# Where the moving operands begin in their partition: another place in each of five rounds of x and in both perceptrons

## The reference, cut to what matters

```python
def sq_relu_mlp(h, w_up, w_down):
    return jnp.square(jax.nn.relu(h @ w_up)) @ w_down

x = x + mix
x = x + sq_relu_mlp(rms_norm(x, norm_mlp_g[layer]), mlp_w_up[layer], mlp_w_down[layer])
```

## Time and profile before

| | |
|---|---|
| Median of three runs | 860.49 us (859.25 to 860.76) |
| The profiled execution's own time | 859.15 us |
| Its span | 857.3 us |
| TensorE busy | 851.0 us, 99% |
| VectorE busy | 652.8 us, 76% |
| ScalarE busy | 496.0 us, 58% |
| Instructions | 17572, of which 7192 matmuls |

### The profile page before, as it was taken

How to read it: one execution, slowest core, us unless ns; L and a number is a source line. 1 busy time by engine, 2 the same in 40 slices (tenths; PEclk the granted TensorE clock), 3 DMA queues, 4 the chain that set the end, 5 groups by cost and what they waited for, 6 DMA issues and landing times.

```text
span 857.3 us, 17572 instructions
## 1 busy us (share of the span) xinstructions
PE 851.0 (99%) x7192; PEld 832.9 (97%) x7192; DVE 652.8 (76%) x1245; ACT 496.0 (58%) x905; POOL 46.8 (5%) x63
## 2 busy tenths in 40 slices
PE   9999999999999999999999999999999999999998
PEld 8999999999999899989999999999999999999998
DVE  6978678898978688575667555566799899997873
ACT  5785787764435667577778444443546564544650
POOL 0000000000000047000000000031020000000000
DMA  9927877878978623367657855617555323565541
GB/s 301 342 66 242 256 238 259 263 267 274 311 245 277 213 99 99 99 204 238 193 178 221 242 188 197 196 51 185 165 167 183 113 75 99 164 206 191 155 147 50
DMA packets 162864, 164.22 MB, mean 192 GB/s; under 512 B 16816, under 2 KB 159328, under 8 KB 162528
## 3 DMA queue, kind: packets, MB, share of 16 engines
q1 hardware_dynamic: 161696, 162.05, 59.7%
q10 hardware_dynamic: 1088, 1.05, 0.4%
HBM read 162.01 MB, written 2.91 MB: 192 GB/s over the span
## 4 chain that ended last, share of the span: by engine, by line
PE 94%; DVE 3%; ACT 1%; DMA 1%; issue 1%; POOL 0%; ACTq 0%; DVEq 0%
PE ps L316 24%; PE ps L318 24%; PE ps L320 24%; PE ps L442 3%; PE ps L1594 2%; PE ps L1596 2%; PE ps L1592 2%; PE ps L1653 2%; PE ps L459 2%; PE ps L1688 1%; PE ps L1692 1%; PE ps L1690 1%; DVE wl L283 1%; PE ps L1634 1%; PE ps L1643 1%; PE ps L1132 1%
## 5 line engine op out<-in xcount | busy, mean ns | idle before, releaser
L283 DVE TENSOR_TENSOR wl<-raw,wh 128x1024 fp32r<-128x1024 f32 x256 | 309.2, 1224 | 27.9 <-ACT wh L276 27.7
L316 PE MATMUL ps<-xh,wh 128*128 128x256 f32 x1136 | 320.2, 282 | 1.6 <-ACT xh L390 1.6
L318 PE MATMUL ps<-xl,wh 128*128 128x256 f32 x1136 | 315.6, 278 | 0.4
L320 PE MATMUL ps<-xh,wl 128*128 128x256 f32 x1136 | 315.4, 278 | 0.0
L276 ACT ACTIVATE wh<-raw 128x1024 fp32r<-128x1024 f32 x256 | 266.9, 1051 | 69.8 <-PE ps L320 62.5
L316 PEld LDWEIGHTS ps<-xh,wh 128*128 128x128 f32 x1136 | 213.8, 188 | 4.1 <-ACT xh L390 2.0
L318 PEld LDWEIGHTS ps<-xl,wh 128*128 128x128 f32 x1136 | 214.1, 188 | 1.2 <-DVE xl L384 1.0
L320 PEld LDWEIGHTS ps<-xh,wl 128*128 128x128 f32 x1136 | 213.5, 188 | 0.0
L320 PE MATMUL ps<-hh,wl 128*128 128x256 f32 x512 | 141.3, 276 | 0.0
L316 PE MATMUL ps<-hh,wh 128*128 128x256 f32 x512 | 141.3, 276 | 0.0
L318 PE MATMUL ps<-hl,wh 128*128 128x256 f32 x512 | 141.3, 276 | 0.0
(11 more groups left out here) (358 smaller groups left out, 1415.0 us busy)
## 6 DMA issues: line engine op xcount, KB each, us to landing
raw<-in_w_in_dram SPq DMA_DIRECT2D x34, 1024.0 KB, 5.4
raw<-in_mlp_up_dram SPq DMA_DIRECT2D x32, 1024.0 KB, 5.4
raw<-in_mlp_down_dram SPq DMA_DIRECT2D x32, 1024.0 KB, 7.3
aw<-in_w_adaT_dram SPq DMA_DIRECT2D x24, 512.0 KB, 4.8
raw<-in_rec_w_in_dram SPq DMA_DIRECT2D x7, 1024.0 KB, 11.6
raw<-in_att_w_in_dram SPq DMA_DIRECT2D x6, 1024.0 KB, 6.2
raw<-in_rec_w_out_dram SPq DMA_DIRECT2D x4, 1024.0 KB, 5.9
raw<-in_att_w_o_dram SPq DMA_DIRECT2D x4, 1024.0 KB, 5.0
```

What stands on the lines that cost most here:

```text
L283: e.tensor_tensor(parts_of(i)[1], raw_of(i), f32(parts_of(i)[0]), op=ALU.subtract).then_inc(S["wl"], 1)
L316: e.matmul(o, H[:, first + n], xh[:, k], start=start and n == 0, stop=False)
L318: e.matmul(o, H[:, first + n], xl[:, k], start=False, stop=False)
L320: ins = e.matmul(o, L[:, first + n], xh[:, k], start=False, stop=stop and n == len(ks) - 1)
```

## The change: what it does

`XH` and `XL` become five pairs of tiles, one for each round, and `HH`, `HL` get a place of their own in each layer. The pairs lie over each other in the same region, which has 512 bytes more. A round's two parts begin at 480, 96, 288, 352 and 224 within 512, the squared rows at 160 in layer 0 and at 416 in layer 1. All tiles that are placed behind move by 512 bytes. The order of instructions, the waits and the sizes are as before.

```diff
+X_AT = (480, 96, 288, 352, 224)
+HIDDEN_AT = (160, 416)
...
     align(top)
-    XH = place("xh", [128, 8, 256], F32R)
-    XL = place("xl", [128, 8, 256], F32R)
+    XH, XL = [], []
+    for r, past in enumerate(X_AT):
+        at_x = [top[0] + (past - top[0]) % 512]
+        XH.append(place(f"xh{r}", [128, 8, 256], F32R, at=at_x))
+        XL.append(place(f"xl{r}", [128, 8, 256], F32R, at=at_x))
+    top[0] += 16384 + 512
...
-        e.activation(XH[:, t], X[:, t], ACT.Copy, scale=gain).then_inc(S["xh"], 1)
+        e.activation(XH[r][:, t], X[:, t], ACT.Copy, scale=gain).then_inc(S["xh"], 1)
...
-            product(e, q, name, o, XH, XL, *of_x(0))
+            product(e, q, name, o, XH[0], XL[0], *of_x(0))
...
-    at_h = [ARENA]
-    HH = [place("hh0", [128, 32, 256], F32R, at=at_h)]
-    HL = [place("hl0", [128, 32, 256], F32R, at=at_h)]
-    at_h = [ARENA]
-    HH.append(place("hh1", [128, 32, 256], F32R, at=at_h))
-    HL.append(place("hl1", [128, 32, 256], F32R, at=at_h))
+    HH, HL = [], []
+    for l, past in enumerate(HIDDEN_AT):
+        at_h = [ARENA + (past - ARENA) % 512]
+        HH.append(place(f"hh{l}", [128, 32, 256], F32R, at=at_h))
+        HL.append(place(f"hl{l}", [128, 32, 256], F32R, at=at_h))
...
-        product(e, q, f"up{l}.{f}", o, XH, XL, *of_x(1 + 2 * l))
+        product(e, q, f"up{l}.{f}", o, XH[1 + 2 * l], XL[1 + 2 * l], *of_x(1 + 2 * l))
...
-        product(e, q, name, main(q, *freed)[:, 0:256], XH, XL, *of_x(2))
+        product(e, q, name, main(q, *freed)[:, 0:256], XH[2], XL[2], *of_x(2))
...
-        product(e, q, name, main(q, *freed)[:, 0:256], XH, XL, *of_x(4))
+        product(e, q, name, main(q, *freed)[:, 0:256], XH[4], XL[4], *of_x(4))
```

More of the change, by code:

```diff
@@ L383, in x_low @@
         q.wait_ge(S["xh"], 8 * r + t + 1)
-        e.scalar_tensor_tensor(XL[:, t], X[:, t], gain, f32(XH[:, t]), op0=ALU.mult, op1=ALU.subtract).then_inc(
+        e.scalar_tensor_tensor(XL[r][:, t], X[:, t], gain, f32(XH[r][:, t]), op0=ALU.mult, op1=ALU.subtract).then_inc(
             S["xl"], 1)
@@ L568, in vector_mixer @@
             q.wait_ge(S["xh"], t + 1)
-            e.tensor_tensor(XL[:, t], XG[:, t], f32(XH[:, t]), op=ALU.subtract).then_inc(S["xl"], 1)
+            e.tensor_tensor(XL[0][:, t], XG[:, t], f32(XH[0][:, t]), op=ALU.subtract).then_inc(S["xl"], 1)
         rms_variance(e, q, 0)
@@ L701, in scalar_mixer @@
             q.wait_ge(S["xg"], t + 1)
-            e.activation(XH[:, t], XG[:, t], ACT.Copy).then_inc(S["xh"], 1)
+            e.activation(XH[0][:, t], XG[:, t], ACT.Copy).then_inc(S["xh"], 1)
         q.wait_ge(S["rate"], 1)
@@ L1120, in tensor_q @@
         ks = range(4 * half, 4 * half + 4)
-        product(e, q, f"q{m}", ps[f"q{m}"], XH, XL, *of_x(2), ks=ks, first=4 * half, start=half == 0, stop=half == 1,
+        product(e, q, f"q{m}", ps[f"q{m}"], XH[2], XL[2], *of_x(2), ks=ks, first=4 * half, start=half == 0, stop=half == 1,
                 release=half == 1)
@@ L1468, in hybrid_two_block_kernel @@
     CTX_ROWS = (HCH, HCL, lambda k: (S["hch"], k + 1), lambda k: (S["hcl"], k + 1))
-    X_ROWS = (XH, XL, *of_x(4))
+    X_ROWS = (XH[4], XL[4], *of_x(4))
     V_ORDER = ((0, True), (0, False), (1, True), (1, False))
@@ L1795, in vector_modulated_low @@
         q.wait_ge(S["xh"], 32 + t + 1)
-        e.scalar_tensor_tensor(XL[:, t], T2.of[f"md{t}"][0][:], ADA[:, t:t + 1], f32(XH[:, t]), op0=ALU.add,
+        e.scalar_tensor_tensor(XL[4][:, t], T2.of[f"md{t}"][0][:], ADA[:, t:t + 1], f32(XH[4][:, t]), op0=ALU.add,
                                op1=ALU.subtract).then_inc(S["xl"], 1)
@@ L2087, in scalar_modulated @@
             q.wait_ge(S["mm"], done["up1.31"])
-            e.activation(XH[:, t], T2.of[f"md{t}"][0][:], ACT.Identity, bias=ADA[:, t:t + 1]).then_inc(S["xh"], 1)
+            e.activation(XH[4][:, t], T2.of[f"md{t}"][0][:], ACT.Identity, bias=ADA[:, t:t + 1]).then_inc(S["xh"], 1)
     def scalar_values2(e, q, n, blk):
```

## The result

The changed kernel took 872.60 us (median of four runs, 872.30 to 874.09), the kernel before 859.87 us beside it (859.12 to 860.76). The ratio is 1.0152, with a 95% interval of 1.0137 to 1.0166: 12.7 us slower. The forecast was 860.5 us with a range up to 868.0; the time lies outside it. The profiled execution took 872.43 us, its span is 870.6 us against 857.3.

The account below looks back on a forecast made before the run. It took TensorE's matmul pace to bound the kernel. Its terms, nothing for work on moved tiles and no pace change, summed to 0 us, so it forecast the median, 860.5 us, range 857.0 to 868.0.

Parts of the forecast that it names:

- What bounds the kernel: Whole kernel: TensorE busy 851.0 of 857.3 us, nobody else waited for; how fast matmuls follow each other sets the end.
- Step 1: ScalarE and VectorE writing and reading moved tiles: price nothing, bounds plus or minus 0.6 us.
- Step 2: Pace of the 3600 moved matmuls: three operand relations in the trace show no difference, so 0 us.
- That is a state, set at an entry and kept: In `product`: 113.3 or 117.8 ns between starts is chosen at an interruption and holds until the next.
- what would prove its reading wrong: Pace switching exactly where up products become down products, with no interruption, would mean the place itself sets it.
- Case B: Entries at 105.3 and 426.6 us fall to the slow pace, costing 6.6 or 4.9 us; likeliest 864 to 867; chance 0.33.
- the worst places: Outcomes left outside the range's upper end of 868.0 us, beside both long entries lost together.
- The upper bound of 13.3 us: All moved matmuls run slow: 2990 fast ones lose 4.45 ns each, 13.3 us.
- Case D: Moved matmuls below 113.3 ns, after the transposes' 109 ns; every second one gaining 4.3 ns gives 852.8 us; chance 0.07.
- The 0 us that the prediction drew from it: By the skill's account of engine ports, no place changes the matmul pace, so the sum is 0 us.
- The flag: In `product`: mean matmul length tells the pace without counting, 276 ns fast, 281 slow, anything else a third pace.
- The scatter of the runs: Three runs 1.5 us apart, worth 340 matmuls at the other pace; one entry at 383 us falling otherwise would do.

Follow-up runs that it names:

- the exchanged places: Changed kernel with weight parts at 224 and all streamed parts at 32, distance -192: 878.55 us, ratio 1.0215 to the kernel before.
- one stage at 96: Changed kernel with all moved tiles back at 224 except layer 0's up products at 96: 863.73 us, ratio 1.0050 to the kernel before.
- down products behind fast up products: Changed kernel, all rounds at 224, squared rows at 96 and 160: 866.87 us, ratio 1.0078; at 352 and 288: 867.48 us, 1.0085.

## Why the prediction was wrong

**What bounds the kernel** held. TensorE's matmuls follow each other without a wait before and after, and the whole loss is in their pace.

**Step 1, the work on the moved tiles, at nothing,** held: 509 and 426 ns against 510 and 426.

**Step 2, "Three relations, no difference. Value taken: no change of pace, 0 us", is the step that failed.** It measured 13.3 us of span. Its two supports were weak in the same way. The fp32 products of round 0 don't tell about the float32r ones: they start 216 ns apart at distance 192 and at 128, while `product` has 113.3 and 118.8 there. And `tensor_rows`, whose distance is -192 and whose pace was kept over a border, was taken to speak for `product`. With the distance of -192, `product` is at 117.8 ns in every long stage (the exchanged places). The form with the operands in each other's role has its own map, which no run here draws.

**"That is a state, set at an entry and kept"** is half right. At distance 192 there are two paces, and the pace often turns at an interruption. But the state does not outlive the place: the pace turned within a few matmuls of the border in both directions (one stage at 96; down products behind fast up products). The prediction had named this as what would prove its reading wrong.

The trace of before already spoke against it. The prediction looked at one border between the two forms, at 551.57 us, where the pace was kept. At another, at 634.38 us, slow `tensor_rows` gives way to `product`. The stretches in front of it and behind it, and the border itself:

```profile
600.46:634.38 33.92, 33.92 (x290) 1.00 0.54 176
634.38:639.84 5.46, 5.46 (x50) 1.00 0.59 191
```

```profile
634.26 0.28 PE L1596 MATMUL ps<-wl,xh 128*128 128x256 f32 x1
634.38 0.28 PE L316 MATMUL ps<-xh,wh 128*128 128x256 f32 x1
```

In front, 288 starts (192 of `product`, then 96 of `tensor_rows`) in 33.92 us are 117.8 ns apart; behind, 48 in 5.46 us are 113.8, with the turn inside. There is no gap and no interruption between them. The stretch behind 105.44 us, besides, begins in the fourth up product, so it does not hold the whole of layer 0's up, as the prediction says.

**Case B** was on the right side, and for the wrong reason. It had a throw of the dice, entries at 105 and 427 us falling the other way, with 4.9 or 6.6 us. What happened is its aside, "a single stage whose place lets only the slow pace stand (768) costs 3.4 us", in all stages but round 0. I gave it no weight of its own and let it end outside the range with "the worst places". The upper bound of 13.3 us, all moved matmuls slow, is the measured figure by chance, since it is made of other parts: round 0 stayed as it was, the down halves and the attention went past the slow pace to 118.8 and 119.7 ns, and the unmoved rest gained 0.8. A range that took the stated bound in would have reached 873.8.

**Case D**, a pace below 113.3 ns, was not found at any of twelve distances.

The Trainium skill, "SBUF — State Buffer", section on the two separate sides, says that on the engines' side only the port that VectorE and GpSimd share causes contention. The 0 us that the prediction drew from it disagrees with these runs: a shift of TensorE's weights alone by 64 bytes costs 3.4%. That this is contention at a port is not shown. The Trainium skill, "TensorE: Matmul & The Clock Gate", section on the back-to-back gap, gives an estimate of 109.2 ns for an isolated matmul of 256 columns. No stretch of `product` in these runs shows it.

**The flag.** "The length is a flag that needs no counting" did not hold. The groups by line of the changed kernel, layer 0's up products at 117.8 ns, then its down products at 118.8 ns:

```profile
L323 PE MATMUL ps<-xh,wh 128*128 128x256 f32 x230 | 64.2, 279 | 0.0
```

```profile
L323 PE MATMUL ps<-hh,wh 128*128 128x256 f32 x245 | 68.9, 281 | 0.0
```

A stretch at 117.8 ns had 281 ns before and has 279 here, and a third pace hides behind the same 281. Starts per microsecond are what counts.

**The scatter of the runs.** I read 1.5 us between runs of one kernel as an entry falling the other way. The runs list a mean granted clock each, and most of the scatter goes with it. Of the 41 runs of the kernel before beside the experiments, the seven at 1.0 have a median of 857.1 us, the 14 at 0.998 of 859.4 and the 20 at 0.996 of 860.7. It is not all: one at 1.0 took 860.62, and the profiled execution of before, also at 1.00, 859.15. Entries do fall either way as well. With everything at 480 the profiled execution, at 1.00, took 856.63 us; there 311 matmuls behind 383 us were fast that are slow in the trace of before, 311 x 4.4 ns = 1.4 us. A table of stretches of one disturbed execution (rows at 216 and 232) shows where the clock fell:

```profile
384.00:388.00 4.00, 2.87 (x12) 0.83 0.23 77
388.00:392.00 4.00, 4.00 (x20) 0.50 0.76 232
392.00:396.00 4.00, 4.00 (x30) 0.82 1.07 348
```

Between the attention and layer 1's up products TensorE stands idle for about 1.8 us in pieces (371 to 377 us in the trace of before, 381 to 386.5 us in this one), and in some executions the granted clock then falls to 0.50, that is 1.2 GHz, for some 7 us. The profiled executions of the kernel before and of the changed kernel have 1.00 throughout, so this is in neither of the two tables by stage.

## What to carry to other kernels

When TensorE is never waited for, count its starts per microsecond by stage, and compare with the best stage of the same form; 4% can lie in a table that shows 99% busy everywhere. Where a streamed operand begins relative to the loaded one can set that pace. It has to be tried for the instruction form in question, with one stage as the probe, since neighbours of 8, 16 and 32 bytes and other forms told nothing about it. Here 192 was the only distance at which long stages of `product` ran fast, though not all of them did. A distance found good is kept for every stage of the form, high and low part alike.

## What the runs showed of the hardware that was not expected

- With float32r matmuls of 256 streamed columns back to back on loads of 128, the time from start to start depends on the distance between the two operands' first bytes in the partition: 113.3 ns at 192, 116.7 to 120.1 ns in the long stages at the eleven others tried. 192 too has a slow pace of 117.8, and -192, which lies at 64 modulo 256, has a few fast products of 113.4. 64 bytes on both at once changed nothing (ratio 1.0005).
- It repeats after 256 bytes: 224 and 480, 96 and 352, 160 and 416 are alike.
- It is sharp: 16 bytes to either side of the good distance cost 5.9 and 3.4 ns a matmul, 8 bytes 6.6 or more, where a start off a multiple of 16 may have its own part.
- At distance 192 the pace can turn at an interruption (383 us in the trace of before, from 113.3 to 117.8 ns), and without one where another form gives way (634.38 us there, from 117.8 to 113.3).
- In a repeating pattern of three, one streamed operand at a bad distance slows all three (117.7 ns, not 114.8).
- The granted clock fell to 0.50 for about 7 us behind idle pieces of 1.8 us in all, in some executions of the same program and not in others. Medians are 857.1 us at a mean clock of 1.0 and 860.7 at 0.996.

What sets these numbers inside the chip no run shows. That the reads of the two operands get in each other's way fits the part that distance, period and pattern play, but it was only argued. Why 192 has two paces is open too.
